# Token rows ahead of the first unit of weights, turned chunks ahead of its parts, and 14 warming calls for 30

## The reference

```python
def swiglu(x, w_up, w_down):
    gate, up = jnp.split(x @ w_up, 2, axis=-1)
    return (jax.nn.silu(gate) * up) @ w_down

def first_block(x, meta_tokens, ffn1_w_up, ffn1_w_down, ...):
    meta = jnp.broadcast_to(meta_tokens[None].astype(x.dtype), (bsz, N_META, D_MODEL))
    h = jnp.concatenate([meta, x], axis=1)
    for l in range(DEPTH):
        h = layer_norm(ALPHA * h + 0.5 * swiglu(h, ffn1_w_up[l], ffn1_w_down[l]), ln_g[l, 0], ln_b[l, 0])
        ...
```

## Time and profile before

| | us |
|---|---|
| median of 3 runs | 2740.18 (2739.95 to 2741.45) |
| the profiled execution | 2740.5 |
| its span, from the first to the last instruction | 2738.7 |
| TensorE busy | 2628.1 (96%) |
| VectorE busy | 1952.0 (71%) |
| ScalarE busy | 1632.9 (60%) |
| GpSimd busy | 402.3 (15%) |
| granted TensorE clock, mean | 0.987 of full |

### The profile page before, as it was taken

How to read it: one execution, slowest core, us unless ns; L and a number is a source line. 1 busy time by engine, 2 the same in 40 slices (tenths; PEclk the granted TensorE clock), 3 DMA queues, 4 the chain that set the end, 5 groups by cost and what they waited for, 6 DMA issues and landing times.

```text
span 2738.7 us, 66120 instructions
## 1 busy us (share of the span) xinstructions
PE 2628.1 (96%) x28056; PEld 2193.0 (80%) x28056; DVE 1952.0 (71%) x1870; ACT 1632.9 (60%) x1698; POOL 402.3 (15%) x450
## 2 busy tenths in 40 slices
PE   9999999999999999999999999998999999989998
PEld 7887788888887788897788888788777787786875
DVE  5557575465566665665775565679999999999997
ACT  5445654353356554455654355657877777877776
POOL 3314122121114122102022102023000000000000
PEclk9999999999999999999999999999999999999999
DMA  8773367667544666654477665368999999999997
GB/s 240 177 215 116 91 177 200 173 180 201 159 149 143 178 173 175 197 170 128 125 201 203 180 191 158 117 224 327 402 409 411 407 404 412 403 406 410 404 407 280
DMA packets 591478, 665.73 MB, mean 243 GB/s; under 512 B 24790, under 2 KB 512604, under 8 KB 591228
## 3 DMA queue, kind: packets, MB, share of 16 engines
q1 hardware_dynamic: 589936, 660.80, 71.3%
q0 software_dynamic: 704, 0.59, 0.4%
q10 hardware_dynamic: 588, 0.74, 0.1%
HBM read 661.01 MB, written 1.05 MB: 242 GB/s over the span
## 4 chain that ended last, share of the span: by engine, by line
PE 64%; DVE 14%; DMA 11%; ACT 6%; issue 3%; DVEq 1%; POOLq 0%; ACTq 0%; SPq 0%; POOL 0%
PE ps L2223 18%; PE ps L2224 17%; PE ps L2225 17%; DVE w_lo L1900 5%; DMA y<-in_moe_w_gate 2%; DMA w<-in_moe_w_gate 2%; ACT w_hi L1281 2%; DMA y<-in_moe_w_down 2%; DVE work L1900 2%; ACT ff L1281 2%; DVE ff L1900 2%; DMA mix<-in_moe_w_down 1%; DMA mix<-in_moe_w_gate 1%; DVE w_lo L1386 1%; DMA w<-in_moe_w_down 1%
## 5 line engine op out<-in xcount | busy, mean ns | idle before, releaser
L2223 PE MATMUL ps<-x_hi,w_hi 128*128 128x96 f16 (+2 forms) x5044 | 1082.3, 247 | 16.3 <-issue 4.8
L2224 PE MATMUL ps<-x_lo,w_hi 128*128 128x96 f16 (+2 forms) x5044 | 1081.8, 247 | 7.0 <-issue 7.0
L2225 PE MATMUL ps<-x_hi,w_lo 128*128 128x96 f16 (+2 forms) x5044 | 1081.5, 247 | 4.0 <-issue 4.0
L1386 DVE SCALAR_TENSOR_TENSOR w_lo<-w,w_hi 128x2048 f16<-128x2048 f32 (+4 forms) x338 | 692.2, 2059 | 316.0 <-ACT w_hi L792 314.6
L792 ACT ACTIVATE w_hi<-w 128x2048 f16<-128x2048 f32 (+4 forms) x338 | 561.4, 1670 | 87.8 <-PE ps L2225 70.3
L2223 PEld LDWEIGHTS ps<-x_hi,w_hi 128*128 128x128 f16 x5044 | 496.0, 98 | 72.3 <-issue 15.1
L2224 PEld LDWEIGHTS ps<-x_lo,w_hi 128*128 128x128 f16 x5044 | 495.9, 98 | 54.1 <-issue 9.3
L2225 PEld LDWEIGHTS ps<-x_hi,w_lo 128*128 128x128 f16 x5044 | 495.7, 98 | 49.0 <-issue 6.7
L1900 DVE SCALAR_TENSOR_TENSOR w_lo<-w,w_hi 128x2048 f16<-128x2048 f32 (+1 forms) x92 | 230.5, 2515 | 18.3 <-ACT w_hi L1281 18.0
L2223 PE MATMUL ps<-ff,w_hi 128*128 128x272 f16 (+1 forms) x880 | 243.3, 276 | 0.0
L2224 PE MATMUL ps<-ff,w_hi 128*128 128x272 f16 (+1 forms) x880 | 243.3, 276 | 0.0
(11 more groups left out here) (406 smaller groups left out, 4717.1 us busy)
## 6 DMA issues: line engine op xcount, KB each, us to landing
w<-in_ffn_w_up SPq DMA_DIRECT2D x176, 512.0 KB, 5.1
w<-in_moe_w_down SPq DMA_DIRECT2D x57, 1024.0 KB, 10.3
w<-in_w_in SPq DMA_DIRECT2D x112, 512.0 KB, 4.7
w<-in_moe_w_up SPq DMA_DIRECT2D x33, 1280.0 KB, 14.0
w<-in_moe_w_gate SPq DMA_DIRECT2D x31, 1280.0 KB, 13.2
mix<-in_moe_w_down SPq DMA_DIRECT2D x37, 1024.0 KB, 10.5
w<-in_mix_w_in SPq DMA_DIRECT2D x64, 512.0 KB, 5.0
mix<-in_moe_w_gate SPq DMA_DIRECT2D x22, 1280.0 KB, 13.2
```

The lines of the kernel that those rows point to most:

```text
L1386: vec.scalar_tensor_tensor(k.w_lo[:, s, 0:size], k.w32[:, s, 0:size], WS, k.w_hi[:, s, 0:size], ALU.mult, ALU.subtract).then_inc(k.parts_r ...
L2223: pe.matmul(acc, w_hi, x_hi, start=first, stop=False)
L2224: pe.matmul(acc, w_hi, x_lo, start=False, stop=False)
L2225: return pe.matmul(acc, w_lo, x_hi, start=False, stop=last)
```

## The change

Four edits, all in the first microseconds of the program. SyncE issues the transfer of the token rows ahead of unit 0 of the weights. ScalarE makes the eight copies of turned chunks first and w_hi of unit 0 behind them. VectorE makes the eight casts first and w_lo of unit 0 behind them. TensorE makes 14 warming calls where it made 30.

```diff
-WARM_UP = 30
+WARM_UP = 14
...
     w_up = i["ffn1_w_up"][0]
+    sp.dma_start(k.tokens[:, 1:3, :], i["x"][0].rearrange("(b p) d -> p b d", p=P)).then_inc(k.tokens_loaded, 16)
     slot(0, 0, (KC, P), chunks(w_up, 0, KC, 0, P), (KC, P), chunks(w_up, 0, KC, FF, P))
-    sp.dma_start(k.tokens[:, 1:3, :], i["x"][0].rearrange("(b p) d -> p b d", p=P)).then_inc(k.tokens_loaded, 16)
...
-    split(0, 0, UNIT)
     for c in range(KC):
         act.wait_ge(k.turned, c + 1)
         act.activation(k.h[:, c, :], k.ps[:, 4 + c % 4, 0:T1], ACT.Copy).then_inc(k.turned_out, 1)
+    split(0, 0, UNIT)
     act.drain()
...
-    split(0, 0, UNIT)
     for c in range(KC):
         vec.wait_ge(k.turned_out, c + 1)
         vec.tensor_copy(k.x_hi[:, c, :], k.h[:, c, :]).then_inc(k.x_hi_ready, 1)
+    split(0, 0, UNIT)
     split(1, 0, UNIT)
```

## The result

| | before | changed |
|---|---|---|
| median of 22 runs, us | 2741.03 | 2745.03 |
| ratio of the times, 95% interval | | 1.0014 (1.0008 to 1.0021) |
| the profiled execution, us | 2740.5 | 2745.41 |
| its span, us | 2738.7 | 2743.6 |

Among the 22 times of the kernel before is one of 4488.29 us, a disturbed run; the median does not feel it. The change makes the kernel 4.0 us or 0.14% slower, with an interval from 2.2 to 5.8 us that leaves out zero. The prediction holds such a change, under 0.2%, to be about what can just be told from none. Its forecast was 3.7 us more.

A forecast was written before the change was run, and what follows sets the result against it. TensorE, busy 2628.1 of 2738.7 us, was taken as the bound, so a delay of its first matmuls carries through. Later parts +1.2 us and the low clock +2.5 give +3.7, 2743.9 us; 8-in-10 range 2740.6 to 2746.5.

The forecast's parts named there:

- The first transpose, T: TensorE's first transpose starts at the later of warming's end and x's landing: 6.3 to 7.5 us, 7.0 taken; 10.54 before.
- The 6.6 taken for x: On SyncE's queue, the token rows x, issued at 1.06 us, land at 6.6, the middle of bounds 5.8 to 7.4.
- Unit 0's parts at T + 9.4: ScalarE and VectorE finish unit 0's parts 9.4 us after the first transpose, with 2.64 us taken for w_lo.
- The clock: A 5.1 us idle stretch of TensorE before unit 0 drops it to 1.2 GHz, losing 1.7 to 3.4 us, 2.5 taken.
- The rival of a clock that holds: TensorE keeps full speed through the 5.1 us idle stretch: +0.5 to +1.7 us, 2740.7 to 2741.9; chance 0.17.
- seven of seven: Later in the trace, all seven TensorE idle stretches of 2.9 us or more stand at a fall to 1.2 GHz.
- Unit 1: TensorE begins the second unit of weights at 23.8 us with no wait for its parts; 20.10 before.
- The sum: Whole kernel: +1.2 us without the clock and +2.5 from the clock make +3.7 us.
- no later stage takes it back: Stages behind the opening: TensorE's work is in one line up to the experts, so the opening's delay stays whole.
- 14 calls are too few: Rival: TensorE still at 1.2 GHz when the transposes begin, up to +9.2 us, 2749.4; chance 0.10.
- x keeps its 8.3 us: Rival: x takes as long from issue to landing as before, first transpose at 9.4, 2746.3 us; chance 0.06.
- The small gain: Rival: x lands at 5.8, warming ends there, w_lo takes 2.29 us, clock holds: -0.3 us, 2739.9; chance 0.05.

The follow-up runs named there:

- e1: The changed kernel with 20 more warming matmuls on TensorE between the transposes and unit 0; median 2741.36 us against 2741.28 for the kernel before, ratio 1.0005.
- e2: The kernel before with only the ScalarE and VectorE edits (copies and casts ahead of unit 0's parts); 2747.96 us against 2741.28, ratio 1.0024.
- e7: The changed kernel with 30 warming calls in place of 14; median 2748.18 us against 2741.19 for the kernel before, ratio 1.0028.
- e8: The changed kernel with nothing altered, profiled a second time; span 2743.9 us, against 2743.6 in its first profile.
- e10: The changed kernel with nothing altered, profiled a third time; span 2742.6 us, against 2743.6 in its first profile.
- e9: The kernel before with nothing altered, profiled a third time; span 2739.6 us, against 2738.7 in its first profile.
- e4: The kernel before with nothing altered, profiled a second time; span 2738.7 us, the same as in its first profile.
- e6: The changed kernel with unit 0's parts made behind the fifth chunk and 12 more warming calls behind the transposes; 2741.51 us against 2741.19 before, ratio 1.0001.
- e3: The kernel before with only 14 warming calls in place of 30; median 2744.32 us against 2741.28, ratio 1.0012.
- e5: The kernel before with only the SyncE edit, token rows ahead of unit 0; median 2742.57 us against 2741.19, ratio 1.0006.

## Why the prediction was right, point by point

**The first transpose, T.** Right: 7.0 was taken, 7.02, 7.38 and 6.76 were measured. The warming set it, as the later of two events; its end moved with the step of the clock, as priced. The last of the three landings that the transposes wait for came at 6.8, so that the transfers left the warming 0.2 us of room. What I had not seen is that this last one need not be x, as the meta rows, on ScalarE's queue, also wait behind it.

```profile
mix<-in_meta_tokens ACTq DMA_DIRECT2D x1, 64.0 KB, 5.6
```

That is a row of the transfers issued in the first 1.25 us of the changed kernel (KB, us to landing); it was 3.8 before. The profile matches the landings on the shared semaphore to the issues in order, so that the row can't tell which of the three landed at 6.8. The packets of each queue can tell more: ScalarE's queue moves the meta rows between 3 and 4 us before, and between 5.2 and 5.8 us in the changed kernel. The packets of x are over by about 5.4 us there. Before, the first half of unit 0 landed 1.1 us behind its last packet (4.7 and 5.76) and x 1.2 us behind its own (9.3 and 10.50). By that x landed near 6.5, an estimate, and the landing at 6.8 is the meta rows'. The 6.6 taken for x fits this. The 5.5 that the prediction estimated from the Trainium skill's figures is about 1 us early by it. It makes no difference while the warming is later.

**Unit 0's parts at T + 9.4.** The direction was right and the size off by 0.5 us: T + 8.91 in the first profile, and 8.91 to 8.92 in e1, e2, e7, e8 and e10. The term that was mis-sized is w_lo at 2.64 us "with the same cover": it took 2.29. ScalarE has no drain ahead of w_hi of unit 0, so w_lo starts at T + 6.56 and not T + 6.86, where the prediction had allowed 0.1 us for this, and that turns round who is first. A row on GpSimd's x_lo (ns least/median/most, first and last start):

```profile
L2142 POOL TENSOR_TENSOR x_lo<-h,x_hi x8: 701/752/2782, 8.5 to 13.7; 128x272 f16<-128x272 f32 x8
```

Before, x_lo of the last chunk had started at 17.1 when VectorE's w_lo started at 17.40 and took 0.35 us more. Now w_lo starts at 13.58, x_lo of the last chunk behind it, and that one takes 2782 ns and not 752, while w_lo takes its undisturbed 2.29. Nobody waits for that last x_lo yet. Unit 1's w_lo, which follows on VectorE, takes 2.79 us beside it, and is over at 18.6, long before TensorE wants it. The Trainium skill (SBUF — State Buffer, "SBUF: two separate sides") says the two engines share a pair of ports that one instruction holds whole, and that the later one is blocked until it ends; the trace agrees, with 2.0 us of waiting.

**The clock.** Right in kind: the idle stretch was 4.62 us (5.1 forecast), the clock fell in all three profiles, and 4.0 us of work ran at 1.2 GHz (4.4 and 3.7 in e8 and e10). The loss is 6.82 less 4.87, 1.95 us (2.15 and 1.81), where I took 2.5 from a range of 1.7 to 3.4. The rival of a clock that holds is out, and e1 shows what it would have been worth. The "seven of seven" on which this step rests holds for every idle stretch of 3.3 us or more in the three profiles of each kernel. Shorter ones are not so regular: after 3.25 us in e9 (to 1976.20) the clock stayed up, while those of 2.34 us in e4 (to 2301.65) and 2.21 us in e8 (to 2524.95) stand at a fall. The 4.6 us here are well clear of that.

**Unit 1.** Forecast 23.8, measured 22.75, 23.31 and 22.36: 2.3 to 3.2 us late against the first profile of before, where 3.7 was the sum. Its own wait is gone, as forecast, and w_hi of unit 1 did wait 0.29 us for its transfer without TensorE feeling it.

**The sum.** 3.7 forecast and 4.0 measured agree better than their terms. The early terms came out 0.8 us smaller; about 1 us came from a place that the forecast held at nothing: the prediction says that "no later stage takes it back", which is so, but it left out that the low clock of later stages may add. That step was not argued from a row, and the right total owes something to chance.

**The other rivals.** That 14 calls are too few did not happen here: in the changed kernel the transposes took 4.30 us, as before, so the clock was up ahead of them. The room is small: in e6 the 28 passes took 6.22 us, which is what 28 slow ones take (28 x 0.22), and the clock had risen only by their end. A fallen clock ahead of the transposes is real where work does not follow at once (e3). That x keeps its 8.3 us did not happen: all was landed by 6.8. The small gain asked for a T of 5.8 and a clock that holds, and had neither. e6 made unit 0's parts earlier instead, at no measurable gain.

## What to carry to other kernels

Find out which of two inputs of a product is late before moving one ahead of the other: the tokens were 3.5 us sooner, and the weights' parts, put behind them on two engines, turned the wait round and made it longer. Count an idle stretch of TensorE twice, for its length and for the slow work behind it (4.6 us and some 2 us here), and where it can't be closed, try to fill it with matmuls that nobody reads (e1). The number of warming calls belongs to the landing of what follows: too few leave a hole (e3), and those too many delay the first product by their own time (e7).

## What the runs showed of the hardware that I had not expected

- The order in which a VectorE and a GpSimd instruction start decides which of them waits. GpSimd 0.3 us ahead cost VectorE's w_lo 0.35 us; VectorE 0.1 us ahead cost GpSimd's x_lo 2.0 us.
- Runs of one kernel lie up to 7.6 us apart (2736.3 to 2743.9 before, in the session of e5 to e7), and part of it is the stretches of low clock in the attention stages, of 3.4 or 6.8 us in one and the same kernel (e9 has one of each). One pair of profiles told 4.9 us, of which 2.3 are that: a change of this size needs several profiles.
- The length of an idle stretch alone does not say whether the clock falls: 3.25 us left it up (e9), and 2.34 and 2.21 us stand at a fall (e4, e8). All of 3.3 us and more do.
- 28 warming passes took from 4.76 to 6.22 us in six executions, by when the clock stepped up.
